# A diff-attention step in another order: scores of pairs 0 and 1 in block 4, of pair 2 in block 5, turns 0 and 1 and outputs 0 in block 5, turns in two banks

## The reference

```python
DIFF_HEADS = 8       # each with two query/key heads of 64 and values of 128
Q_BLOCK = 128

def diff_attention(h, w_in, w_out, lam, subln_g, lambda_init, pos):
    q, k, v = jnp.split(h @ w_in, 3, axis=-1)
    q = partial_rope(q.reshape(B, S, 2 * H, Dh), pos).reshape(B, S, H, 2, Dh)
    k = partial_rope(k.reshape(B, S, 2 * H, Dh), pos).reshape(B, S, H, 2, Dh)
    v = v.reshape(B, S, H, DIFF_V_DIM)
    lam_full = jnp.exp(jnp.sum(lam[0] * lam[1])) - jnp.exp(jnp.sum(lam[2] * lam[3])) + lambda_init
    def chunk(i):
        sc = jnp.einsum('bqhcd,bkhcd->bhcqk', qc, k) * scale
        p = masked_probs(sc, pos[None, :] <= qpos[:, None])
        a = p[:, :, 0] - lam_full * p[:, :, 1]
        return jnp.einsum('bhqk,bkhe->bqhe', a, v)
    o = rms_norm(chunked(chunk, S // Q_BLOCK), subln_g, 1e-5) * (1.0 - lambda_init)
    return o.reshape(B, S, H * DIFF_V_DIM) @ w_out
```

## Time and profile before

| | us |
|---|---|
| median of 3 runs | 2844.03 |
| lowest, highest | 2842.75, 2844.04 |
| the profiled execution, its own time | 2843.54 |
| its span in the trace | 2841.7 |
| PE busy | 2786.0 |
| DVE busy | 1854.6 |
| ACT busy | 1535.3 |

### The profile page before, as it was taken

How to read it: one execution, slowest core, us unless ns; L and a number is a source line. 1 busy time by engine, 2 the same in 40 slices (tenths; PEclk the granted TensorE clock), 3 DMA queues, 4 the chain that set the end, 5 groups by cost and what they waited for, 6 DMA issues and landing times.

```text
span 2841.7 us, 34706 instructions
## 1 busy us (share of the span) xinstructions
PE 2786.0 (98%) x13354; PEld 2272.1 (80%) x13354; DVE 1854.6 (65%) x2702; ACT 1535.3 (54%) x2658; POOL 189.7 (7%) x302
## 2 busy tenths in 40 slices
PE   9999999999999999999999999999999999999997
PEld 7887788888888888876888888788788788787786
DVE  6766776676667667666776766677655755646654
ACT  6547654654765465456655546665444444444442
POOL 1010100000000000014001001100100000000000
PEclk9999999999999999999999999999999999999999
DMA  8665467566446756651676675367555565655652
GB/s 260 230 218 178 147 217 249 188 222 229 164 151 213 252 186 222 227 184 60 198 241 215 213 260 188 105 229 241 207 192 192 196 190 188 208 179 174 189 184 89
DMA packets 358661, 559.40 MB, mean 197 GB/s; under 512 B 15681, under 2 KB 245057, under 8 KB 358241
## 3 DMA queue, kind: packets, MB, share of 16 engines
q1 hardware_dynamic: 350752, 535.02, 56.7%
q0 software_dynamic: 7600, 21.81, 2.3%
q10 hardware_dynamic: 144, 0.36, 0.0%
HBM read 556.03 MB, written 1.10 MB: 196 GB/s over the span
## 4 chain that ended last, share of the span: by engine, by line
PE 93%; DVE 4%; ACT 1%; issue 1%; POOL 1%; DMA 0%; DVEq 0%; ACTq 0%; POOLq 0%
PE ps L689 39%; PE ps L754 26%; PE ps L695 20%; PE ps L659 4%; PE ps L834 1%; PE ps L865 1%; DVE LO L1802 1%; ACT SB L1535 1%; DVE XL L1843 0%; POOL ST L2400 0%; PE ps L875 0%; ACT JUNK L1397 0%; DVE M L1881 0%; DVE M L1920 0%; PE ps L842 0%
## 5 line engine op out<-in xcount | busy, mean ns | idle before, releaser
L689 PE MATMUL ps<-HI,XH 128*128 128x512 f32 x2480 | 985.2, 397 | 3.8 <-DVE LO L1802 1.4
L689 PE MATMUL ps<-LO,XH 128*128 128x512 f32 x2480 | 969.6, 391 | 0.0
L1802 DVE TENSOR_TENSOR LO<-RAW,HI 128x1024 fp32r<-128x1024 f32 x468 | 567.3, 1223 | 334.7 <-ACT HI L1377 331.5
L695 PE MATMUL ps<-HI,XL 128*128 128x512 f32 x2480 | 767.9, 391 | 0.4
L1807 DVE SCALAR_TENSOR_TENSOR LO<-RAW,GC,HI 128x512 fp32r<-128x512 f32 (+1 forms) x896 | 623.6, 746 | 188.9 <-ACT HI L1384 186.5
L1377 ACT ACTIVATE HI<-RAW 128x1024 fp32r<-128x1024 f32 x468 | 490.6, 1059 | 442.8 <-PE ps L754 289.1
L1384 ACT ACTIVATE HI<-RAW,GC 128x512 fp32r<-128x512 f32 (+1 forms) x896 | 587.8, 714 | 153.8 <-PE ps L695 129.3
L695 PEld LDWEIGHTS ps<-HI,XL 128*128 128x128 f32 x2480 | 465.0, 188 | 107.0 <-DVE XL L1843 8.0
L689 PEld LDWEIGHTS ps<-HI,XH 128*128 128x128 f32 x2480 | 467.0, 188 | 102.3 <-issue 2.9
L689 PEld LDWEIGHTS ps<-LO,XH 128*128 128x128 f32 x2480 | 467.3, 188 | 92.3
L754 PE MATMUL ps<-HI,AH 128*128 128x512 f32 x880 | 273.6, 392 | 0.0
(11 more groups left out here) (203 smaller groups left out, 2014.3 us busy)
## 6 DMA issues: line engine op xcount, KB each, us to landing
RAW<-in_ffn_w_in SPq DMA_DIRECT2D x350, 512.0 KB, 4.7
RAW<-in_ffn_w_out SPq DMA_DIRECT2D x88, 1024.0 KB, 5.0
RAW<-in_w_ada SPq DMA_DIRECT2D x48, 1024.0 KB, 5.1
RAW<-in_w_in SPq DMA_DIRECT2D x44, 1024.0 KB, 5.1
RAW<-in_w_ffn_in SPq DMA_DIRECT2D x88, 512.0 KB, 4.8
RAW<-in_diff_w_in SPq DMA_DIRECT2D x24, 1024.0 KB, 5.1
RAW<-in_w_ffn_out SPq DMA_DIRECT2D x22, 1024.0 KB, 5.0
RAW<-in_moba_w_in SPq DMA_DIRECT2D x12, 1024.0 KB, 5.2
```

Of the source, the lines that this page charges most:

```text
L689: e.matmul(ps[:, b + t, 0:nw], XH[:, k, t * P:(t + 1) * P], q[s][:, c * nw:(c + 1) * nw], start=(k == 0 and q is HI), stop=False)
L695: i = e.matmul(ps[:, b + t, 0:nw], XL[:, k, t * P:(t + 1) * P], HI[s][:, c * nw:(c + 1) * nw], start=False, stop=(k == 7))
L1802: e.tensor_tensor(LO[n % NSPLIT][:, 0:w], RAW[t.buf][:, at[1] * w:(at[1] + 1) * w], HI[n % NSPLIT][:, 0:w].bitcast(F32), ALU.subtract).the ...
```

## The change

Only the diff steps' order is changed, and one bank; moba gets functions of its own with the order it had. No instruction is added or removed.

- Pairs 0 and 1 have their scores in block 4, in front of quarters 1 and 3, both into banks 6 and 7; pair 2 in block 5, in front of quarter 1.
- Turn 0 stands in front of quarter 2 of block 5, turn 1 and outputs 0 in front of quarter 3.
- Turn i goes to bank 4 for even and 5 for odd i, and waits for the copy of turn i-2.
- In the tail PE begins with the scores of pairs 3 and 4, then turn 2 and outputs 1, and goes on by rounds as before.
- ACT does exps 0 and 1 in front of block 4's copy, exps 2, the copies of turns 0 and 1 and sums 0 in front of block 5's copy.
- DVE does maxima 0 in front of the rotation of block 3, maxima 1 and 2 and differences 0 to 2 between the splits, and in the tail difference i, maxima i+2, in place i-3.

```diff
+        def diff_bank_of(i):
+
+            return 6 if i < 2 else 2 * ((i + 1) % 2)
...
             def probs_turned(st, i, nj):
 
                 SB = st.t["SB"]
-                if i >= 1:
-                    e.wait_ge(s_pt, st.c["pt"] + i)
+                free = i - (0 if nj == 2 else 1)
+                if free >= 1:
+                    e.wait_ge(s_pt, st.c["pt"] + free)
                 for j in range(nj):
-                    o = turn(ps[:, 4 + j, :], [SB[:, i % 3, j, c * P:(c + 1) * P] for c in range(3)])
+                    o = turn(ps[:, 4 + (j if nj == 2 else i % 2), :], [SB[:, i % 3, j, c * P:(c + 1) * P] for c in range(3)])
...
+            def pair_mixed(st, i):
+
+                c, TM, diff = st.c, st.t["TM"], st.kind == "diff"
+                e.wait_ge(s_pt, c["pt"] + i + 1)
+                if i >= 2:
+
+                    e.wait_ge(s_o, c["o"] + (2 * (i - 1) if diff else i - 1))
+                if diff:
+                    v = lambda j, kt: TM[:, kt, 2048 + i * P:2048 + (i + 1) * P]
+                else:
+                    v = lambda j, kt: TM[:, kt, 2048 + (2 * i + j) * 64:2048 + (2 * i + j + 1) * 64]
+                outputs(st, i, st.t["PT"], i % 2, 6 + i % 2, 1 if diff else 2, P if diff else 64, v)
...
+            def diff(st):
+                c = st.c
+                def in_values(n, k2):
+                    if (n, k2) == (4, 1):
+                        e.wait_ge(s_tn, c["tn"] + 6)
+                        pair_scores(st, 0)
+                    elif (n, k2) == (4, 3):
+                        e.wait_ge(s_ex, c["ex"] + 1)
+                        pair_scores(st, 1)
+                    elif (n, k2) == (5, 1):
+                        e.wait_ge(s_cp, c["cp"] + 5)
+                        pair_scores(st, 2)
+                    elif (n, k2) == (5, 2):
+                        e.wait_ge(s_tn, c["tn"] + 8)
+                        e.wait_ge(s_df, c["df"] + 1)
+                        probs_turned(st, 0, 1)
+                    elif (n, k2) == (5, 3):
+                        e.wait_ge(s_df, c["df"] + 2)
+                        probs_turned(st, 1, 1)
+                        e.wait_ge(s_ex, c["ex"] + 2)
+                        pair_mixed(st, 0)
+                for n in range(6):
+                    if n == 0:
+                        first_block(st, 512)
+                    else:
+                        later_block(st, n, 512, (lambda k2, n=n: in_values(n, k2)) if n >= 4 else None)
+                    if 1 <= n <= 4:
+                        turns_of_qk(st, n - 1)
+                for i in range(1, 8):
+                    if i + 2 < 8:
+                        e.wait_ge(*((s_cp, c["cp"] + 6) if i == 1 else (s_ex, c["ex"] + i + 1)))
+                        pair_scores(st, i + 2)
+                    if i == 7:
+                        last_pairs(st)
+                    if i >= 2:
+                        e.wait_ge(s_df, c["df"] + i + 1)
+                        probs_turned(st, i, 1)
+                        pair_mixed(st, i - 1)
+                pair_mixed(st, 7)
+                heads_out(st)
...
                 e.wait_ge(s_pf, st.c["pf"] + i + 1)
                 if i >= 2:
                     e.wait_ge(s_mix, st.c["mix"] + i - 1)
-                e.activation(st.t["PT"][:, i % 2, 0:nj, :], ps[:, 4:4 + nj, 0:384], ACT.Copy).then_inc(s_pt, 1)
+                b = 4 if nj == 2 else 4 + i % 2
+                e.activation(st.t["PT"][:, i % 2, 0:nj, :], ps[:, b:b + nj, 0:384], ACT.Copy).then_inc(s_pt, 1)
...
+                for n in range(6):
+                    if n == 4:
+                        e.wait_ge(s_lam, c["lam"] + 2)
+                        e.activation(LS[:, 2:4], LS[:, 0:2], ACT.Exp).then_inc(s_lex, 1)
+                        split(st.w0 + 22)
+                        exps(st, 0, diff_bank_of(0))
+                        split(st.w0 + 24)
+                        exps(st, 1, diff_bank_of(1))
+                    elif n == 5:
+                        split(st.w0 + 26)
+                        exps(st, 2, diff_bank_of(2))
+                        split(st.w0 + 27)
+                        probs(st, 0, 1)
+                        split(st.w0 + 28)
+                        probs(st, 1, 1)
+                        sums(0)
+                    if n >= 1:
+                        split(st.w0 + 4 * n + 9)
+                    block_of_heads(st, n)
+                for i in range(1, 8):
                     if i == 7:
                         outputs_high(st, 0)
-                    probs(st, i, 1 if diff else 2)
+                    if i >= 2:
+                        probs(st, i, 1)
                     if i + 2 < 8:
-                        exps(st, i + 2, bank_of(i + 2))
-                    if diff and i >= 1:
+                        exps(st, i + 2, diff_bank_of(i + 2))
+                    if i >= 2:
                         sums(i - 1)
-                if diff:
-                    sums(7)
+                sums(7)
                 outputs_out(st)
...
-                for n in range(5):
-                    projected(st, n, TM, n * 512, 512 if n < 4 else 0)
+                for n in range(3):
+                    projected(st, n, TM, n * 512, 512)
                 e.wait_ge(s_mixw, c["mixw"] + 32)
                 e.tensor_scalar(SGN[:, :], SGN[:, :], 1.0 - linit, None, ALU.mult).then_inc(s_sgn, 1)
                 e.tensor_tensor(LM[:, 0:4:2, :], LM[:, 0:4:2, :], LM[:, 1:4:2, :], ALU.mult).then_inc(s_lam, 1)
                 e.wait_ge(s_lam, c["lam"] + 1)
                 e.tensor_reduce(LS[:, 0:2], LM[:, 0:4:2, :], AX.X, ALU.add).then_inc(s_lam, 1)
-                maxima(st, 0, bank_of(0))
-                split(st.w0 + 27)
-                maxima(st, 1, bank_of(1))
+                split(st.w0 + 21)
+                maxima(st, 0, diff_bank_of(0))
+                projected(st, 3, TM, 3 * 512, 512)
+                split(st.w0 + 23)
+                maxima(st, 1, diff_bank_of(1))
...
                 difference(0)
+                split(st.w0 + 25)
+                maxima(st, 2, diff_bank_of(2))
                 difference(1)
+                split(st.w0 + 28)
+                difference(2)
                 projected(st, 5, TM, 0, 0)
-                maxima(st, 2, bank_of(2))
-                maxima(st, 3, bank_of(3))
-                for i in range(2, 8):
+                maxima(st, 3, diff_bank_of(3))
+                maxima(st, 4, diff_bank_of(4))
+                for i in range(3, 8):
                     difference(i)
-                    if i >= 3:
-                        in_place(i - 3)
+                    if i + 2 < 8:
+                        maxima(st, i + 2, diff_bank_of(i + 2))
+                    in_place(i - 3)
                     if i == 7:
                         outputs_low(st, 0)
-                    if i + 2 < 8:
-                        maxima(st, i + 2, bank_of(i + 2))
                 for i in range(5, 8):
                     in_place(i)
                 outputs_out(st)
```

More of the change, by code:

```diff
@@ L942, in hook, with last_pairs, heads_out, moba @@
+            def last_pairs(st):
+                e.wait_ge(s_ex, st.c["ex"] + 8)
+                outputs_flipped(st, 0, 8 if st.kind == "diff" else 4)
+            def heads_out(st):
                 def hook(k, t):
                     if (k, t) == (3, 0):
-                        outputs_flipped(st, 1, 16 if diff else 8)
+                        outputs_flipped(st, 1, 16 if st.kind == "diff" else 8)
                     last_hook(st, k, t, 8)
                 rows_of_outputs(st, st.w0 + 24, hook, s_end0)
-            def diff_or_moba(st):
+            def moba(st):
+                c = st.c
@@ L965, in diff_or_moba @@
                         turns_of_qk(st, n - 1)
-                softmax_attention(st)
+                for i in range(8):
+                    if i + 2 < 8:
+                        e.wait_ge(*((s_cp, c["cp"] + 5 + i) if i < 2 else (s_ex, c["ex"] + i + 1)))
+                        pair_scores(st, i + 2)
+                    if i == 0:
+                        e.wait_ge(s_ex, c["ex"] + 2)
+                    if i == 7:
+                        last_pairs(st)
+                    e.wait_ge(s_ex, c["ex"] + i + 1)
+                    probs_turned(st, i, 2)
+                    if i >= 1:
+                        pair_mixed(st, i - 1)
@@ L1355, in _ @@
                 else:
-                    diff_or_moba(st)
+                    (diff if st.kind == "diff" else moba)(st)
         @block.scalar
@@ L1552, in outputs_out, with block_of_heads, moba @@
                 split(st.w1 + 2)
-            def diff_or_moba(st):
-                c, TM, QT, KT = st.c, st.t["TM"], st.t["QT"], st.t["KT"]
-                diff = st.kind == "diff"
+            def block_of_heads(st, n):
+                copy_out(st, n, st.t["TM"][:, :, n * 512:(n + 1) * 512], 2 * ((n + 1) % 2), 512)
+                if 1 <= n <= 4:
+                    X, scale = (st.t["QT"], SCALE) if n < 3 else (st.t["KT"], 1.0)
```

(22 more changed lines are left out.)

48 lines of the change are left out of this document (17 added, 31 removed).

## The result

| | kernel before | changed kernel |
|---|---|---|
| median of 5 runs beside each other, us | 2844.03 (2842.75 to 2844.63) | 2856.17 (2853.31 to 2857.68) |
| ratio, 95% interval | 1 | 1.0042 (1.003 to 1.0054) |
| profiled execution, us (its span) | 2843.54 (2841.7) | 2856.17 (2854.3) |
| PE's granted clock, mean of the span | 0.997 | 0.995 |

The account below looks back on a forecast made before the run. PE bounds the kernel, working 2786.0 of 2841.7 us. Blocks 2.95 plus tail 1.45 make 4.4 us a step, twice +8.8, giving 2852.8 us on the median; range 2849.0 to 2855.5.

Parts of the forecast that it names:

- (a): Blocks 4 and 5: scores, two turns and outputs moved in cost 2.95 us a step, bounds 2.58 to 3.39.
- the third rival: Blocks: PE stands still waiting for ACT or DVE; if 2 us later than that, 2856.8 us; chance 0.06.
- (b): Tail's start: PE waits for block 5's copy until T+1.43, about as before; almost nothing won.
- (c): First exp in the tail: pair 3's exps at T+3.78, pair 5's scores at T+5.56, its maxima at T+6.86.
- T: The moment at which block 5 is done; 273.46 in step 1 of the kernel before.
- (d): DVE's tail order, maxima ahead of in place: two rounds of 4.01 us, outputs 4 at T+16.76 against T+14.38.
- The ring: Tail: outputs, scores, maxima, in place wait in a circle; 4.01 us a pair in place of 2.77, for pairs 6 and 7.
- The first rival: Tail: the ring doesn't hold, rounds take 2.77 us; +3.8 us in all, 2847.8; chance 0.10.
- (e): Tail's end, same work as before: outputs 5 at T+18.60, w_out rows at T+23.78 against T+22.33, 1.45 us later.
- (f): Turns in two banks, each waiting for the copy of turn i-2: gains nothing in the tail.
- The rival on the other side: Pairs fed ahead: tail loses two rounds of 2.77 us; -2.6 a step, -5.2 in all, 2838.8 us; chance 0.04.
- Its dearest case: Blocks' cost at 3.39 us and a ring of 4.2: 5.3 us a step, 2854.6 us.

Follow-up runs that it names:

- e4: e1 with pair 3's scores in banks 2 and 3, no longer waiting for block 5's copy: 2844.19 us, ratio 1.0002 to the kernel before.
- e1: The changed kernel with DVE's in place put back ahead of the maxima, as in the kernel before: 2846.7 us, ratio 1.0011 to before.
- e2: The kernel before with only DVE's order changed, maxima i+2 ahead of in place i-3: 2849.53 us, ratio 1.002.
- e0: The changed kernel itself, unaltered, run again in a second job: 2854.73 us, ratio 1.0042 to the kernel before.
- e6: The changed kernel plus two unread 384-column matmuls in front of each of outputs 2, 3 and 4 in diff steps: 2851.52 us, ratio 1.0028 to before.
- e9: e6 with one added matmul in place of two in front of each of outputs 2, 3 and 4: 2851.31 us, ratio 1.0029 to before.
- e3: The changed kernel with all turns back in one bank (4), each waiting for the previous turn's copy: 2857.33 us, ratio 1.0041 to before.
- e10: The kernel before with only DVE's in place of pair 5 moved ahead of the low halves of M's first half: 2842.76 us, ratio 0.9997.

## Why the prediction was right in its sign and wrong in its size

(a) **The blocks.** 2.75 us a step in place of 2.95, nearer to the lower bound of 2.58. The bare starts are the better price here: scores, two turns and outputs cost 0.17 us more than themselves. PE had no hole there, so the third rival, standing still in the blocks, did not come about.

(b), (c) **The start.** Pair 3's scores came at T+1.51 (T+1.43 predicted), its exps at T+3.93 (T+3.78), pair 5's scores at T+5.70 (T+5.56). The hole in front is 1.36 us and is put down to ACT's copy of TM, as expected. e4 shows the same step from the other side.

(d) **The ring.** 4.02 and 4.01 us for a worked out 4.01; outputs 2 at T+8.88 (T+8.74) and outputs 4 at T+16.91 (T+16.76). Of the 0.15 us 0.09 is T itself, which the prediction took at the first scores, 273.46, and not at 273.37; the rest is the way from maxima to exps in (c), 1.12 us for 1.05. e1 takes the order away and the ring goes; e2 brings it alone, and the ring comes. The first rival, in which the ring doesn't hold, falls by both.

(e) **The end.** Outputs 5 at T+18.75, against T+18.60, in step 1 of the changed kernel's profile and of e0's alike. The tail was to be 23.78 us, and without a fall of the clock it is: 23.83 in e0, 23.70 in e6, where PE does 3.9 us more. In the profiled execution it is 24.79 and 26.39, which is 0.96 and 2.56 over e0's, 3.5 us together. **This is the step that failed.** (e) took the way from outputs 5 to the rows of w_out at its old length, since "both stretches hold the same work as before", and (d) took each round of the ring at 4.01: a tail with PE at 2.43 of 4 us was taken to run at the clock that the earlier trace rows show for one with PE at 18.02 of 22.33. The sum had no term for the clock, and had each matmul at the duration that it had had. In the ring's last rounds the matmuls are no longer of that duration. In step 1 outputs 5 took 1.62 us in place of 0.91, and the flip came 1.42 us behind them in place of 0.74; in step 10 one round took 5.47 us in place of 4.01 as well.

The terms with the clock left out: (2.75 + 1.41) x 2 = 8.3 us, for the 8.8 of the forecast. e6 (+7.6) and e9 (+7.9) stand a little below. With the 3.5 us of the clock it is the 11.8 of the account above. The median of the changed kernel's runs is 12.1 above before in one job and 11.0 in the other, so the fall of the clock is worth 3 to 5 us, and up to 9 in a single run (2860.1 less 2851.3).

Here a section of the Trainium skill bears on the row, which the prediction had not weighed. "TensorE: Matmul & The Clock Gate", section "A second HAM failure mode: psum-queue depth-cycling", tells of a kernel that cycles through PSUM banks in each iteration and in which the array idles for short times between groups of matmuls, often enough for the clock to swing between its levels. The trace agrees: a wait of 1.6 us for a bank in each round, and 0.50 in the row of 294 to 296; e0's step 1, with the same waits and a clock of 1.00, shows that it need not happen each time. By that rule the ring of (d) was a reason to give the lower clock a chance of its own, and the ring was in the prediction.

(f) **The banks.** Nothing, as forecast; e3 has one fewer and no other time that could be told.

**The rival on the other side**, that the pairs are fed ahead, had 4 in 100 and needed pair 3's exps to be as early as pair 1's were, for two rounds of 2.77 us. e4 goes half the way: with these at T+2.50, where pair 2's stood before (T+2.44), the tail shrinks by 2.57 us, about one round, where more than 2.75 was wanted, and the result is no change. Whether the second round could be won was not tried. The advice of the Trainium skill to interleave, weighed there, held only as far as the tail shrank; the stretch that took the work had no hole to give.

The range was too narrow upward because all cases in it kept every matmul at its old speed. (Its dearest case adds up to 5.2 us a step, 3.39 + 1.45 + 0.38, and not to 5.3, which changes nothing here.) What isn't settled is why the clock falls in one step and not in the other of the same execution, and so what share it has in the next run. Nor does the fall need the ring: it came once without (e10, step 10).

## What to carry to other kernels

When an engine runs in order, write down for each bank who frees it and what stands ahead of that on the freeing engine. A ring of one round's length in place of two is found on paper, as here, to 0.01 us. Then ask what PE's new holes do to its clock: a forecast that lengthens a stretch by holes, and keeps the matmuls' durations from a fuller stretch, can come out too low. Work moved out of a stretch with holes into one without pays only if the stretch shrinks by more than the work, so restore the cover that was moved, or move less.
